# MLP w2 by seven block products per slab (Strassen–Winograd) in six of eight slabs, all modulation pieces in the w1 phase, and a fifth weight slot

## The reference, cut to what matters

```python
def squared_relu_mlp(x, w1, w2):
    return jnp.square(jax.nn.relu(x @ w1)) @ w2          # 1024 -> 4096 -> 1024

x = layer_norm(DN_ALPHA * x + squared_relu_mlp(x, mlp_w1[i], mlp_w2[i]), ln2_g[i], ln2_b[i])

# second model, for each of its layers l
mod = silu(c) @ ada_w[l] + ada_b[l]                      # 1024 -> 6144, one row
```

## Time and profile before

| | |
|---|---|
| median of 3 runs | 2394.42 us (2393.16 to 2395.58) |
| profiled execution, its own time | 2395.37 us |
| span of that profile, first to last instruction | 2393.5 us |
| TensorE busy | 2355.0 us, 98% of the span |
| VectorE busy | 873.5 us, 36% |
| ScalarE busy | 426.4 us, 18% |
| DMA, mean over the span | 281 GB/s |
| granted TensorE clock, mean | 0.994 of full speed |

### The profile page before, as it was taken

The page is one execution under the profiler, slowest core; times in us unless marked ns, Lnnn a source line. Parts: engine busy times, 40 slices in busy tenths (PEclk is TensorE's granted clock), DMA queues, the critical chain, the costliest instruction groups (busy, mean ns, idle before and its releaser), DMA issues.

```text
span 2393.5 us, 24299 instructions
## 1 busy us (share of the span) xinstructions
PE 2355.0 (98%) x10366; PEld 1398.3 (58%) x10366; DVE 873.5 (36%) x1711; ACT 426.4 (18%) x967; POOL 75.4 (3%) x130
## 2 busy tenths in 40 slices
PE   8999999999999999999899999999999999999998
PEld 5578447875586448787444444434878644444443
DVE  3455426667345334363211222212345322112112
ACT  3410003356110011220111111101122011111111
POOL 2000000010100000000000000000000000000000
PEclk9999999999999999999999999999999999999999
DMA  7367745354477743236799999993225589999995
GB/s 281 125 228 298 280 182 197 142 188 164 179 295 266 307 147 144 108 148 274 313 427 428 426 428 428 427 419 151 107 92 228 231 361 428 428 427 427 427 427 238
DMA packets 57433, 671.54 MB, mean 281 GB/s; under 512 B 7312, under 2 KB 7600, under 8 KB 18528
## 3 DMA queue, kind: packets, MB, share of 16 engines
q1 hardware_dynamic: 50160, 649.45, 67.0%
q0 software_dynamic: 7152, 20.39, 2.5%
HBM read 666.56 MB, written 3.26 MB: 280 GB/s over the span
## 4 chain that ended last, share of the span: by engine, by line
PE 96%; DVE 2%; DMA 1%; issue 0%; POOL 0%; ACT 0%; SPq 0%; DVEq 0%; POOLq 0%; ACTq 0%
PE ps L101 93%; DVE arena L117 1%; PE ps L321 1%; DMA arena<-ssm_rows 1%; PE ps L2333 1%; DVE arena L114 0%; DMA ring<-in_attn_w_in 0%; PE ps L2315 0%; PE ps L591 0%; PE ps L1590 0%; DVE arena L110 0%; PE ps L1060 0%; DVE X L117 0%; POOL small L117 0%; ACT arena L106 0%
## 5 line engine op out<-in xcount | busy, mean ns | idle before, releaser
L101 PE MATMUL ps<-arena 128*64 128x512 f32 (+5 forms) x3408 | 754.8, 453 | 5.5 <-DVE arena L117 3.7
L101 PE MATMUL ps<-ring,arena 128*64 128x512 f32 (+1 forms) x2112 | 684.3, 593 | 0.0
L101 PE MATMUL ps<-XTGB,ring 128*128 128x256 f32 x2800 | 618.6, 380 | 0.0
L101 PEld LDWEIGHTS ps<-XTGB,ring 128*128 128x128 f32 x2800 | 527.6, 190 | 78.7 <-issue 5.9
L101 PEld LDWEIGHTS ps<-arena 128*64 128x64 f32 (+2 forms) x3408 | 370.1, 166 | 310.5 <-issue 292.9
L101 PEld LDWEIGHTS ps<-ring,arena 128*64 128x64 f32 (+1 forms) x2112 | 253.1, 155 | 359.2 <-issue 358.4
L117 DVE TENSOR_TENSOR arena<-ps,arena 128x512 f32<-128x512 f32 (+4 forms) x166 | 96.0, 613 | 376.0 <-PE ps L101 363.6
L101 PE MATMUL ps<-ring,XTGB 128*128 128x512 f32 (+3 forms) x568 | 226.5, 557 | 0.4 <-DMA ring<-in_attn_w_in 0.3
L101 PEld LDWEIGHTS ps<-ring,XTGB 128*128 128x128 f32 x568 | 106.0, 192 | 113.3 <-issue 107.8
L105 ACT ACTIVATE arena<-ps 128x512 f32<-128x512 f32 (+1 forms) x81 | 47.6, 594 | 651.5 <-PE ps L101 651.5
L117 DVE TENSOR_TENSOR arena<-arena,ps 128x512 f32<-128x512 f32 x32 | 22.0, 688 | 388.0 <-PE ps L101 388.0
(11 more groups left out here) (136 smaller groups left out, 807.9 us busy)
## 6 DMA issues: line engine op xcount, KB each, us to landing
ring<-in_exp_w SPq DMA_DIRECT2D x88, 2048.0 KB, 19.5
arena<-in_exp_w SPq DMA_DIRECT2D x80, 2048.0 KB, 18.5
ring<-in_mlp_w SPq DMA_DIRECT2D x32, 2048.0 KB, 7.8
ring<-in_ada_w SPq DMA_DIRECT2D x24, 2048.0 KB, 8.2
XTGB<-in_exp_w SPq DMA_DIRECT2D x20, 2048.0 KB, 18.8
ring<-in_ssm_w_in SPq DMA_DIRECT2D x12, 2048.0 KB, 7.8
ring<-in_w_in SPq DMA_DIRECT2D x12, 2048.0 KB, 7.9
ring<-in_gate_w SPq DMA_DIRECT2D x12, 2048.0 KB, 7.9
```

The costliest lines, as they stand in the source:

```text
L101: return self.e.matmul(o, lhsT=lhsT, rhs=rhs, start=start, stop=stop, skip_group_check=True)
```

## The change

The w2 product of slabs 0 to 5 is done by seven block products in place of eight. `hT` of a slab is seen as 2x2 blocks a11..a22 (token half by pair of chunks), the weight slab as b11..b22 (pair of chunks by column half). VectorE forms four sums of a blocks (`S`, 128x256 each) and four of b blocks (`T`, 128x1024 each) for each slab in `block_sums`. TensorE then makes seven products of two matmuls each, in the order 1, 2, 3, 5, 7, 6, 4, into seven held banks that add up over the six slabs. `blocks_out` combines the seven banks into X, with one copy of bank 1 by ScalarE. Slabs 6 and 7 go the old way; `add_rows` adds them without the factor ALPHA, which `blocks_out` has applied. The sums take the places of the accumulators, of `h0`, and of `ab` and `modc`; the modulation must be finished by then, so all its pieces move into the w1 phase, two for most steps, and a fifth ring slot (the end of the arena) is added while the MLP loads its weights.

```diff
-        def piece_at(l, n):
-
-            s = n - l
-            return s if 0 <= s < 13 else None
+        PIECES = [(0,), (1, 2), (3, 4), (5, 6), (7, 8), (9, 10), (11,), ()]
...
         def ada_pe(pe, l, n, acc):
...
+            for r in range(3):
+                if n == 0 or 4 * r + 3 not in PIECES[n - 1]:
+                    continue
+                ps = bank(pe, "ada", l, hold=True) if r == 0 else ps_of("ada", l)
+                pe.wait_ge(at("consts"), *[at("ada", l, 4 * r + j) for j in range(4)])
...
+        NS = 6
+        ORDER = (1, 2, 3, 5, 7, 6, 4)
...
         def mlp_sp(sp, l):
+            ring.tenant[NRING + 4] = ("so", 3) if l else "ao1"
+            ring.turn.append(NRING + 4)
             for s in range(8):
                 slab(sp, ("m1", l, s), "mlp_w1", (l * 8 + s) * P * SLAB, 8, 512)
-                if s < 7:
-                    ada_sp(sp, l, s)
+                ada_sp(sp, l, s)
             for s in range(8):
                 slab(sp, ("m2", l, s), "mlp_w2", (l * 8 + s) * P * SLAB, 4, 1024)
-                ada_sp(sp, l, 7 + s)
+            ring.turn.remove(NRING + 4)
...
                 else:
+                    ada_pe(pe, l, s, acc)
                     gemm_f(pe, ("m1", l, s), ("m1", l, s), 4)
...
-                if s < 7:
-                    ada_pe(pe, l, s, acc)
-            ps = [bank(pe, "mo", l, q, hold=True) for q in range(4)]
+            for s in range(NS):
+                a11, a12, a21, a22 = blocks_a(hT, s)
+                b11, b12, b21, b22 = blocks_b(l, s)
+                s1, s2, s3, s4_ = sA[s % 2]
+                t1, t2, t3, t4 = sB
+                pairs = {1: (a11, b11), 2: (a12, b21), 3: (s4_, b22), 4: (a22, t4), 5: (s1, t1), 6: (s2, t2), 7: (s3, t3)}
+                pe.wait_ge(at("w", ("m2", l, s)), at("h", l, s))
+                for k in ORDER:
+                    ps = ps_of("P", l, k) if s else bank(pe, "P", l, k, hold=True)
+                    a, b = pairs[k]
+                    if k == 3:
+                        pe.wait_ge(at("S", l, s))
+                    if k >= 4:
+                        pe.wait_ge(at("T", l, s, k))
+                    for c in range(2):
+                        ins = pe.mm(ps, a[:, c, :], b[:, c, :], s == 0 and c == 0, s == NS - 1 and c == 1)
...
-            for s in range(6):
-                ada_pe(pe, l, 7 + s, acc)
-                for q in range(4):
-                    out(s, q)
-            ada_pe(pe, l, 13, acc)
...
+        def block_sums(v, l, s, hT, sA, sB):
...
+            if s == 1:
+                v.wait_ge(at("mod", l))
+            if s >= 2:
+                v.wait_ge(at("P done", l, s - 2, 6))
+            k = v.then_inc(v.tt(s1, a21, a22, ALU.add), ("S", l, s))
...
+            v.wait_ge(at("w", ("m2", l, s)), at("P done", l, s - 1, 5) if s else at("ada mm", l, 2))
+            k1 = v.then_inc(v.tt(t1, b12, b11, ALU.subtract), ("T", l, s, 5))
...
+            v.wait_ge(k2, at("P done", l, s - 1, 4) if s else None)
+            v.then_inc(v.tt(t4, t2, b21, ALU.subtract), ("T", l, s, 4), ("free", ("m2", l, s)))
...
         def mlp_dve(v, l, hT, acc, ab, sA, sB, sU):
             for s in range(8):
+                if s == 7:
+                    ada_dve(v, l, s, acc, ab)
+                    block_sums(v, l, 0, hT, sA, sB)
...
+            for s in range(1, NS):
+                block_sums(v, l, s, hT, sA, sB)
+            blocks_out(v, l, sU)
```

More of the change, by code:

```diff
@@ L364, in build, with add_rows @@
         lrs = small[:, 28:30]
-        def add_rows(v, key, t):
+        def add_rows(v, key, t, scale=True):
             for h in range(2):
@@ L753, in attn_dve @@
             norm_rows_all(v, 1, at("gb", "ln1"))
-        def piece_at(l, n):
-            s = n - l
-            return s if 0 <= s < 13 else None
+        PIECES = [(0,), (1, 2), (3, 4), (5, 6), (7, 8), (9, 10), (11,), ()]
         def ada_sp(sp, l, n):
-            s = piece_at(l, n)
-            if s is not None and s < 12:
+            for s in PIECES[n]:
                 slab(sp, ("ada", l, s), "ada_w", (l * 12 + s) * P * SLAB, 8, 512)
         def ada_dve(v, l, n, acc, ab):
[L770 to L773, removed]
+            for s in PIECES[n]:
                 w = weights(("ada", l, s))
@@ L791, in ada_pe @@
         def ada_pe(pe, l, n, acc):
[L792 to L802, removed]
+            for r in range(3):
[3 more added lines that the diff above has]
+                pe.wait_ge(at("consts"), *[at("ada", l, 4 * r + j) for j in range(4)])
+                for j in range(4):
+                    ins = pe.mm(ps[32 * j:32 * j + 3, :], C["e12"][:, 11 - r:14 - r], acc[(4 * r + j) % 8], r == 0, r == 2)
+                pe.then_inc(ins, ("ada mm", l, r))
+                if r == 2:
+                    banks.drop(("ada", l))
         def ada_b_pool(pool, l, ab):
@@ L807, in ada_b_pool, with blocks_a, blocks_b, mlp_pe @@
                 pool.landed(pool.e.dma_start(ab[32 * j:32 * j + 3, :], rows[j]), "ada_b", ("ada_b", l))
+        NS = 6
+        ORDER = (1, 2, 3, 5, 7, 6, 4)
+        READ = (1, 2, 3, 5, 6, 7, 4)
+        def blocks_a(hT, s):
+            return [hT[:, 4 * s + 2 * k:4 * s + 2 * k + 2, t * P:(t + 1) * P] for t in range(2) for k in range(2)]
+        def blocks_b(l, s):
+            w = weights(("m2", l, s))
+            return [w[:, 2 * k:2 * k + 2, n * 512:(n + 1) * 512] for k in range(2) for n in range(2)]
         def mlp_sp(sp, l):
+            ring.tenant[NRING + 4] = ("so", 3) if l else "ao1"
+            ring.turn.append(NRING + 4)
             for s in range(8):
                 slab(sp, ("m1", l, s), "mlp_w1", (l * 8 + s) * P * SLAB, 8, 512)
-                if s < 7:
-                    ada_sp(sp, l, s)
+                ada_sp(sp, l, s)
             for s in range(8):
                 slab(sp, ("m2", l, s), "mlp_w2", (l * 8 + s) * P * SLAB, 4, 1024)
-                ada_sp(sp, l, 7 + s)
-        def mlp_pe(pe, l, n, hT, h0, acc, turn_0):
+            ring.turn.remove(NRING + 4)
+        def mlp_pe(pe, l, n, hT, h0, acc, turn_0, sA, sB):
             for s in range(8):
@@ L832, in mlp_pe @@
                         turn(pe, ("h0", l), t, lambda c: h0[:, t, c * P:(c + 1) * P], 4, at("relu 0", l, t))
-                if s < 7:
-                    ada_pe(pe, l, s, acc)
-            ps = [bank(pe, "mo", l, q, hold=True) for q in range(4)]
+            for s in range(NS):
[14 more added lines that the diff above has]
+                        ins = pe.mm(ps, a[:, c, :], b[:, c, :], s == 0 and c == 0, s == NS - 1 and c == 1)
+                    pe.then_inc(ins, ("P done", l, s, k), *([("free", ("m2", l, s))] if k == 3 else []),
+                                *([("P", l, k)] if s == NS - 1 else []))
+            for k in READ:
+                banks.drop(("P", l, k))
+            ps = [bank(pe, "mo", l, 0, hold=True)] + [None] * 3
             def out(s, q, before_2=None):
                 w = weights(("m2", l, s))
+                if s == NS and q:
+                    ps[q] = bank(pe, "mo", l, q, hold=True)
                 pe.wait_ge(at("w", ("m2", l, s)), at("h", l, s))
@@ L844, in out @@
                     ins = pe.mm(ps[q], hT[:, 4 * s + c, t * P:(t + 1) * P], w[:, c, n_ * 512:(n_ + 1) * 512],
-                                s == 0 and c == 0, s == 7 and c == 3)
+                                s == NS and c == 0, s == 7 and c == 3)
                 if q == 3:
@@ L862, in mlp_pe, with mlp_act @@
                 banks.drop(("mo", l, q))
-        def mlp_act(act, l, hT, h0):
+        def mlp_act(act, l, hT, h0, sU):
             for t in range(2):
@@ L879, in mlp_act @@
                                      ("h", l, 0), ("read", "h0", l, t, 0))
-        def mlp_dve(v, l, hT, acc, ab):
+            act.wait_ge(at("P", l, 1))
+            act.then_inc(act.cp(sU, ps_of("P", l, 1)), ("P1", l), ("read", "P", l, 1))
+        def block_sums(v, l, s, hT, sA, sB):
+            a11, a12, a21, a22 = blocks_a(hT, s)
+            b11, b12, b21, b22 = blocks_b(l, s)
+            s1, s2, s3, s4_ = sA[s % 2]
+            t1, t2, t3, t4 = sB
+            v.wait_ge(at("h", l, s))
+            if s == 1:
[3 more added lines that the diff above has]
+            k = v.then_inc(v.tt(s1, a21, a22, ALU.add), ("S", l, s))
+            v.wait_ge(k)
+            k = v.then_inc(v.tt(s2, s1, a11, ALU.subtract), ("S", l, s))
+            v.then_inc(v.tt(s3, a11, a21, ALU.subtract), ("S", l, s))
+            v.wait_ge(k)
+            v.then_inc(v.tt(s4_, a12, s2, ALU.subtract), ("S", l, s))
+            v.wait_ge(at("w", ("m2", l, s)), at("P done", l, s - 1, 5) if s else at("ada mm", l, 2))
+            k1 = v.then_inc(v.tt(t1, b12, b11, ALU.subtract), ("T", l, s, 5))
+            if s:
+                v.wait_ge(at("P done", l, s - 1, 7))
+            v.then_inc(v.tt(t3, b22, b12, ALU.subtract), ("T", l, s, 7))
+            v.wait_ge(k1, at("P done", l, s - 1, 6) if s else None)
+            k2 = v.then_inc(v.tt(t2, b22, t1, ALU.subtract), ("T", l, s, 6))
```

(47 more changed lines are left out.)

23 lines of the change are left out of this document (15 added, 8 removed).

## The result

The changed kernel takes 2431.76 us (median of 4 runs, 2431.28 to 2433.39) where the kernel before takes 2394.82 (4 runs beside them). The ratio is 1.0156, 95% interval [1.0139, 1.0174]: 36.9 us slower. The forecast was 2431.

What follows compares the result with a forecast made beforehand. TensorE was taken as the bound, busy 2355.0 of 2393.5 us. Waits 45.6 plus clock 10.8 less products 20.7 gave +35.7 on 2395.4, 2431 us for a median; the range 2420 to 2444 should hold 8 times in 10.

Steps and rivals of the forecast that it cites:

- part 5: w1 phase: narrow modulation matmuls wait for pieces behind the squares; six times 7.6 us idle plus 1.8 us low clock.
- The rival by the whole throttled time: At the six waits, low-clock time counts whole, idle or not: 7.3 us each, half lost; 2442 us, 10%.
- the row at 1622: Kernel before: TensorE idle 3.73 us around 1618, clock low about 1622.2 to 1625.7, 1.8 us lost; taken against skill's formula.
- part 1: w2 phase: 14 matmuls for 16 in six slabs of two layers, 24 fewer; 20.7 us saved on TensorE.
- part 2: w2 phase: VectorE's block sums, 6.6 us a slab beside 12.1 us of TensorE, hidden by margins of about 9 us; cost 0.
- part 4: w1 phase: twenty slab loads instead of fifteen; w1 slab 3 half a microsecond late, covered by the wait; cost 0.
- the first rival: w1 phase: pieces ready when the slab before ends, so no waits and only the products' saving stays; 2374.7 us, 4%.

Runs made afterwards that it cites:

- mid24: Changed kernel with the narrow modulation matmuls placed after 24 of the 32 w1 matmuls of slabs 3, 5 and 7; 2385.23 us.
- fill8: Changed kernel with eight 128x512 matmuls, whose result nobody reads, ahead of each of the six waits; 2419.46 us.
- oldw2: Changed kernel with all eight w2 slabs done the old way, without block sums; 2452.09 us.
- order24_oldw2: `mid24` with each w1 slab's load one piece earlier on the SP queue and all eight w2 slabs the old way; 2399.30 us.
- order24_twice: `mid24` with each w1 slab's load one piece earlier on the SP queue and each b sum made twice; 2379.52 us, against 2378.42 without the doubling.
- mid8: Changed kernel with the narrow modulation matmuls after 8 of the 32 w1 matmuls, loads in the changed kernel's order; 2407.36 us.

## Why the prediction was right

It was right in its number, 2431 for 2431.8, and by its own steps, with one gap. The terms that make up the sum are each near what was measured (waits 45.6 for 44.9, clock 10.8 for 13.2, products 20.7 for 21.2). The clock is the largest error, 2.4 us, and half of it is hidden by the other two. Two of its readings of rows were wrong, and are put right below; neither is a term of the sum.

- **The waits** (part 5): 7.6 us each forecast from five rows. The first measures 7.55, from slab 2's end at 160.19 + 13.84 = 174.03 to 181.58, and five others about 7.46. `mid24` takes the cause away and the six waits are gone.
- **The clock** (part 5): 1.8 us forecast, 2.05 by `fill8`, 9.69 - 7.49 = 2.2 from the rows. A little low: the first wait of a layer loses 0.84 in the narrow group and 1.85 in the matmuls, the third only 0.84 and 0.92 (14.77 us from 260.50 to 275.27, for 13.85). The windows of the changed kernel answer to the earlier trace rows; in the first wait the clock falls at about 176.9, 2.8 us after the last matmul, and is back at 187.2, 5.6 us after the narrow matmuls begin:

```profile
176.00:177.00 1.00, 0.00 (x0) 0.96 1.04 442
177.00:178.00 1.00, 0.00 (x0) 0.50 0.99 426
...
187.00:188.00 1.00, 1.00 (x6) 0.92 1.00 426
```

  The prediction says that the clock fell after about 4 us without matmuls at both places. That holds for the one at 1622. At the other, 0.60 over the window from 1151 puts the fall at 1151.2, and the last matmul had ended at 1149.20 + 1.08 = 1150.28, 0.9 us earlier; but TensorE had work for only 1.5 of the 3 us from 1147 to 1150 as well:

```profile
1149.20 1.08 PE L101 MATMUL ps<-XTGB 128*128 128x36 f32 x8 [0.78 <-DVE XTGB L122]
```

- **The rival by the whole throttled time.** The clock is low for 10.2 us in this wait, and half of that would be 5.1 us where 2.7 were lost. In the second it is low for 6.8 us, 3.4 against 2.1. The clock is already low for 4.7 and 2.6 us of these while TensorE has nothing to do. Only the rest counts: 5.6, 4.3 and 3.6 us of low clock with TensorE at work in the three waits, of which half is 2.8, 2.1 and 1.8, where 2.7, 2.1 and 1.8 were lost. The rule of the Trainium skill (TensorE: Matmul & The Clock Gate, Terms), penalty as throttled time by one minus the ratio, gives 1.6 to 1.9 times the loss here, and the trace disagrees with it for these holes. The prediction brought the row at 1622 against the same rule, and that was a misreading: there the matmuls begin at 1621.98 and the clock falls at 1622.24, so nearly all of the 3.4 us of low clock has TensorE at work, and half of it, 1.7 us, is about the 1.8 lost. At that place rule and trace agree.
- **The products** (part 1): 20.7 forecast; 21.2 by the rows, 20.3 by `oldw2`, 20.9 by `order24_oldw2`. A matmul between them takes 12.02 / 14 = 0.859 us, so the waits between the products of a slab cost nothing.
- **The sums** (part 2): 0 forecast, and 0 found. T4 of slab 1 starts at 287.56 and ends at 288.79, 1.5 us after the slab began, for a need at 10.3, as worked out. `order24_twice` bears the margin out.
- **The loads** (part 4): 0 was right for this kernel, and for the stated reason that the wait of part 5 covers them, but only slab 3 was named as late without it. In `mid24` six of the eight late slabs are others. This is the step that was mis-sized. I had worked out the issue times of slabs 4 to 7 with the waits in and not without. It did not touch the forecast, but the first rival, 2374.7 with the waits gone, was 10.5 us too fast: 2385.2 was measured, and 2378.4 with the loads reordered as well.

A wait that falls away thus gave 46.5 us and not 58, because something else had been late behind it. When a stall is priced, the question of what is late next has to be asked of the timeline without the stall.

## What to carry to other kernels

When a consumer on the bottleneck engine is put directly behind its own last producer chain, it stands for the whole chain, however idle the other engine is on average: look up what must end before the awaited instruction can *begin*, not how busy its engine is. Moving the consumer behind 24 matmuls of independent work made a change that loses 1.6% into one that gains 0.4%, and it gained 0.7% once the loads, which the stall had hidden, were reordered so that the weight slabs wait less for slots that the slower engine frees. Strassen's seven products for eight paid here in float32 on TensorE, as the sums fitted beside them on VectorE: they saved 20 to 21 us of 24 x 0.86 us.

## What the runs showed of the hardware

In the six holes of the changed kernel the granted clock fell from 2.4 to 1.2 GHz 2.6 to 4.7 us after the last matmul and came back 3.6 to 5.6 us after work began. What it cost was half of the low time in which TensorE worked, 1.8 to 2.8 us a hole, and not half of all the low time. In `mid8` it fell at holes of only 2.42 and 2.15 us (3.7 us of work and a hole of 1.21 and 1.48 ahead of them), when TensorE had already been working again for 1.0 and 1.2 us; after a hole of 2.05 us behind one of 1.55 it did not fall. So a hole can be paid for after it has closed. The row at 1622 had shown it already in the kernel before, and I had not seen it there. Matmuls whose result nobody reads, put into the six holes of 7.4 us, bought back 12.3 us of 2431.8 (`fill8`).
